# A packed square of attention probabilities for the second block of queries

## The reference

```python
nb = s // WINDOW                      # 2 blocks of 128 queries
kcat = concatenate([previous key block (zeros for the first), own key block])
scores = einsum('bnqkrd,bnjkd->bkrnqj', qb, kcat) * HEAD_DIM ** -0.5
dist = qi - kj + WINDOW
valid = (dist >= 0) & (dist < WINDOW) & (key_pos >= 0)
logits = where(valid, scores - slope * dist, -inf)
m = maximum(max(logits), sink)
pexp = exp(logits - m)
probs = pexp / (sum(pexp) + exp(sink - m))
out = einsum('bkrnqj,bnjkd->bnqkrd', probs, vcat)
```

## Time and profile before

| | us |
|---|---|
| median of 3 runs | 1937.97 (1937.92 to 1938.11) |
| the profiled execution | 1938.91 |
| its span | 1937.2 |
| TensorE busy | 1922.5 (99%) |
| VectorE busy | 1264.7 (65%) |
| ScalarE busy | 1084.3 (56%) |
| mean granted TensorE clock | 0.999 |

### The profile page before, as it was taken

How to read it: one execution, slowest core, us unless ns; L and a number is a source line. 1 busy time by engine, 2 the same in 40 slices (tenths; PEclk the granted TensorE clock), 3 DMA queues, 4 the chain that set the end, 5 groups by cost and what they waited for, 6 DMA issues and landing times.

```text
span 1937.2 us, 28994 instructions
## 1 busy us (share of the span) xinstructions
PE 1922.5 (99%) x10281; PEld 1634.9 (84%) x10281; DVE 1264.7 (65%) x1534; ACT 1084.3 (56%) x1474; POOL 33.5 (2%) x79
## 2 busy tenths in 40 slices
PE   9999999999999999999999999999999999999998
PEld 7888888888887878888888888888888888888886
DVE  6777788777868975545444555776776666744454
ACT  6566765777557764444344445666666666534443
POOL 1000000000000100000000000000000000000000
PEclk9999999999999999999999999999999999999999
DMA  7765666666654437666666565666666666666564
GB/s 225 211 191 166 197 205 183 186 174 204 195 163 131 131 123 215 194 190 197 194 191 194 178 228 192 200 188 186 191 189 193 186 184 189 190 200 194 193 195 142
DMA packets 294855, 362.05 MB, mean 187 GB/s; under 512 B 11073, under 2 KB 217985, under 8 KB 293377
## 3 DMA queue, kind: packets, MB, share of 16 engines
q1 hardware_dynamic: 294784, 361.12, 61.0%
HBM read 358.91 MB, written 2.16 MB: 186 GB/s over the span
## 4 chain that ended last, share of the span: by engine, by line
PE 98%; DVE 1%; ACT 1%; issue 0%; DMA 0%; DVEq 0%; SPq 0%; POOLq 0%; POOL 0%; ACTq 0%
PE ps L1381 35%; PE ps L1383 18%; PE ps L1366 14%; PE ps L1368 13%; PE ps L1367 13%; PE ps L1568 1%; PE ps L1496 1%; PE ps L1509 1%; PE ps L1520 0%; PE ps L1569 0%; PE ps L1557 0%; PE ps L1414 0%; DVE lo L851 0%; ACT hi L438 0%; PE ps L1436 0%
## 5 line engine op out<-in xcount | busy, mean ns | idle before, releaser
L851 DVE TENSOR_TENSOR lo<-raw,hi 128x1024 fp32r<-128x1024 f32 x658 | 801.5, 1224 | 520.3 <-ACT hi L438 514.2
L1381 PE MATMUL ps<-uHL,hi 128*128 128x512 f32 x2960 | 1041.9, 396 | 1.3 <-DVE uHL L863 1.0
L438 ACT ACTIVATE hi<-raw 128x1024 fp32r<-128x1024 f32 x658 | 688.7, 1055 | 519.6 <-PE ps L1368 386.5
L1383 PE MATMUL ps<-uHL,lo 128*128 128x256 f32 x2960 | 828.2, 280 | 0.0
L1381 PEld LDWEIGHTS ps<-uHL,hi 128*128 128x128 f32 x2960 | 554.7, 187 | 132.3 <-issue 5.0
L1383 PEld LDWEIGHTS ps<-uHL,lo 128*128 128x128 f32 x2960 | 558.9, 189 | 0.1
L1368 PE MATMUL ps<-hi,aL 128*128 128x512 f32 x384 | 149.5, 389 | 0.0
L1368 PE MATMUL ps<-hi,hL 128*128 128x512 f32 x352 | 136.9, 389 | 0.0
L1367 PE MATMUL ps<-lo,hH 128*128 128x512 f32 x352 | 136.9, 389 | 0.0
L1366 PE MATMUL ps<-hi,hH 128*128 128x512 f32 x352 | 136.9, 389 | 0.0
L443 ACT ACTIVATE hb<-ps 128x512 f32<-128x512 f32 x92 | 54.7, 595 | 124.1 <-PE ps L1383 124.1
(11 more groups left out here) (189 smaller groups left out, 1647.3 us busy)
## 6 DMA issues: line engine op xcount, KB each, us to landing
raw<-w_in SPq DMA_DIRECT2D x266, 512.0 KB, 4.3
raw<-w_ffn_in SPq DMA_DIRECT2D x176, 512.0 KB, 3.8
raw<-w_ffn_out SPq DMA_DIRECT2D x88, 512.0 KB, 4.3
raw<-w_ssm_out SPq DMA_DIRECT2D x64, 512.0 KB, 4.4
raw<-w_attn_out SPq DMA_DIRECT2D x32, 512.0 KB, 4.2
raw<-w_o SPq DMA_DIRECT2D x32, 512.0 KB, 4.4
rows_b<-cum_rows SPq DMA_DIRECT2D x8, 1024.0 KB, 6.5
x_tok<-x SPq DMA_DIRECT2D x8, 256.0 KB, 5.4
```

Source lines behind the costliest of these rows:

```text
L438: act.activation(hi[:, s % SLOTS, :], raw[:, s % SLOTS, :], ACT.Copy).then_inc(hi_ready, 1)
L851: ve.tensor_tensor(lo[:, s % SLOTS, :], raw[:, s % SLOTS, :], hi[:, s % SLOTS, :].bitcast(F32), ALU.subtract).then_inc(lo_ready, 1)
L1381: pe.matmul(ps[:, pair + c, :], w_hi, uHL[:, kk].rearrange("p a n -> p (a n)"), start=kk == 0, stop=False)
L1383: last = pe.matmul(ps[:, pair + c, 0:SEQ], w_lo, uHL[:, kk, 0, :], start=False, stop=kk == k - 1)
```

## The change

In the second block of queries the two triangles complement each other. After the logits, the element-wise maximum of the previous-key block and the own-key block is written over the previous-key block (masked places lie far below every logit), so one 128x128 square holds all the logits of a row. Maximum, exponential, sum and normalisation work on that square, and so do the transposes: four for six. ScalarE copies the transposed square to `pT`, and VectorE then makes both triangles of it with two multiplies by masks (`att_masks`), before `values`, whose code is unchanged. A new semaphore `pt_kept` leads from ScalarE's copy to VectorE; `pt_ready` now comes from VectorE. `att_masks` of an iteration stands behind `lo_of` of the odd unit: iterations 0, 1 behind units 5, 7, iterations 2, 3 behind units 1, 3 of the next group (9 and 11 at the end). The last `values` moves from before unit 11 to before unit 13, its keep and the last piece of `attn_hi` from units 11 and 13 to 16, and the last pieces of `branch_lo` from units 12 and 13 to 13 and 17.

```diff
@@ att_exps (ScalarE)
-                    act.activation(lg[:, i, j, 0:P], lg[:, i, j, 0:P], ACT.Exp, bias=S[:, 1, 2 * j:2 * j + 1],
-                                   accum_out=S[:, 3, 2 * j:2 * j + 1])
-                    act.activation(lg[:, i, j, P:3 * P], lg[:, i, j, P:3 * P], ACT.Exp, bias=S[:, 1, 2 * j + 1:2 * j + 2],
-                                   accum_out=S[:, 3, 2 * j + 1:2 * j + 2])
+                    for b in range(2):
+                        n = 2 * j + b
+                        act.activation(lg[:, i, j, b * P:(b + 1) * P], lg[:, i, j, b * P:(b + 1) * P], ACT.Exp,
+                                       bias=S[:, 1, n:n + 1], accum_out=S[:, 3, n:n + 1])
@@ att_turned (ScalarE)
-                act.activation(pT[:, i % 2], ps[:, M + 2:M + 4, :].rearrange("p b n -> p (b n)")[:, 0:6 * P],
-                               ACT.Copy).then_inc(pt_ready, 1)
+                act.activation(pT[:, i % 2].rearrange("p (j n) -> p j n", j=2)[:, :, 0:2 * P],
+                               ps[:, M + 2, :].rearrange("p (j n) -> p j n", j=2), ACT.Copy).then_inc(pt_kept, 1)
@@ merge units (ScalarE)
+                elif u == 12:
+                    attn_hi(2)
+                elif u == 16:
                     att_keep(KVH - 1, 3)
-                elif u < 14:
                     act.drain()
-                    attn_hi(u - 10)
+                    attn_hi(3)
@@ VectorE
+            def packed(i):
+                return lg[:, i, :, 0:2 * P].rearrange("p j (b n) -> p j b n", b=2)
+
+            def att_masks(h, i):
+                ve.wait_ge(pt_kept, h * 4 + (i + 1))
+                p = pT[:, i % 2].rearrange("p (j c n) -> p j c n", j=2, c=3)
+                ve.tensor_tensor(p[:, :, 2, :], p[:, :, 1, :], triu[:, None, :].to_broadcast([P, 2, P]), ALU.mult)
+                ve.tensor_tensor(p[:, :, 1, :], p[:, :, 1, :], strict[:, None, :].to_broadcast([P, 2, P]),
+                                 ALU.mult).then_inc(pt_ready, 1)
@@ att_logits (VectorE)
+                ve.tensor_tensor(lg[:, i, :, P:2 * P], lg[:, i, :, P:2 * P], lg[:, i, :, 2 * P:3 * P], ALU.max)
+                ve.drain()
                 mx = pairs(S[:, 0, :])
-                ve.tensor_reduce(mx[:, :, 0:1], lg[:, i, :, 0:P], op=ALU.max, axis=AX.X)
-                ve.tensor_reduce(mx[:, :, 1:2], lg[:, i, :, P:3 * P], op=ALU.max, axis=AX.X)
+                ve.tensor_reduce(mx[:, :, :, None], packed(i), op=ALU.max, axis=AX.X)
@@ att_probs (VectorE)
-                r = pairs(S[:, 5, :])
-                ve.tensor_tensor(lg[:, i, :, 0:P], lg[:, i, :, 0:P], r[:, :, 0:1].to_broadcast([P, 2, P]), ALU.mult)
-                ve.tensor_tensor(lg[:, i, :, P:3 * P], lg[:, i, :, P:3 * P], r[:, :, 1:2].to_broadcast([P, 2, 2 * P]),
+                ve.tensor_tensor(packed(i), packed(i), pairs(S[:, 5, :])[:, :, :, None].to_broadcast([P, 2, 2, P]),
                                  ALU.mult).then_inc(probs_ready, 1)
@@ VectorE's order
+            def att_mask_side(h, u, older=True):
+                if u in (1, 3) and older:
+                    att_masks(h - 1, u // 2 + 2)
+                if u in (5, 7):
+                    att_masks(h, u // 2 - 2)
...
                     att_first(h, u)
                     lo_of(U_Q + u, h * Q_UN)
+                    att_mask_side(h, u)
                     q_rest(h, u)
...
-                if 10 <= u < 14:
-                    i = u - 10
+                if u in (10, 11, 13, 17):
+                    i = (10, 11, 13, 17).index(u)
@@ turn_probs (TensorE)
-                    for c in range(3):
-                        o = (3 * j + c) * P
-                        last = pe.transpose(ps[:, M + 2 + o // 512, o % 512:o % 512 + P],
-                                            lg[:, i, j, c * P:(c + 1) * P], ident[:])
+                    for c in range(2):
+                        o = (2 * j + c) * P
+                        last = pe.transpose(ps[:, M + 2, o:o + P], lg[:, i, j, c * P:(c + 1) * P], ident[:])
@@ merge units (TensorE)
-                    elif u == 11:
+                    elif u == 13:
                         values(KVH - 1, 3)
```

More of the change, by code:

```diff
@@ L230, in build @@
                                                           sem("probs_turned"), sem("pt_ready"))
-        pv_done, attn_out = sem("pv_done"), sem("attn_out")
+        pt_kept, pv_done, attn_out = sem("pt_kept"), sem("pv_done"), sem("attn_out")
         sv_ready, z_scaled, rows_landed, rows_used = sem("sv_ready"), sem("z_scaled"), sem("rows_landed"), sem("rows_used")
@@ L1173, in _ @@
                 lo_of(U_Q + u, 0)
+                att_mask_side(0, u, older=False)
                 if u == 1:
@@ L1212, in _ @@
                 if u < 8:
+                    att_mask_side(KVH - 1, u)
+                elif u in (9, 11):
+                    att_masks(KVH - 1, u // 2 - 2)
+                if u < 8:
                     q_rest(KVH - 1, u)
```

## The result

| | before | after |
|---|---|---|
| median of 22 runs, us | 1938.3 (1937.79 to 1939.16) | 1941.67 (1940.02 to 1942.92) |
| the profiled execution, its span | 1938.91, 1937.2 | 1941.75, 1940.0 |
| granted clock, mean | 0.999 | 0.998 |

The ratio is 1.0016, interval 1.001 to 1.0021: 3.4 us slower. The interval lies clear of 1, but the difference is under the 0.2% (3.9 us) that the prediction names as what this measurement can tell, so it counts as no change. The 22 times of after lie in two groups with nothing between 1940.59 and 1941.10: seven from 1940.02 to 1940.59 and fifteen from 1941.10 to 1942.92. Before has no such gap. The profiled run belongs to the upper one. The mean granted clock of the whole run is 0.999 in all seven runs of the lower group and 0.998 or less in fourteen of the fifteen of the upper one, a value that only 9 of 87 later runs of before show.

The account below looks back on a forecast made before the run. TensorE was taken as the bound, with VectorE saturated. VectorE's 7 x 0.51 = 3.57 us, with -0.05 and -0.03, made +3.5; less 1.1 for transposes, +2.4: 1940.4 us, own range 1939.2 to 1942.2, whole range 1937.2 to 1943.1.

Parts of the forecast that it names:

- part 1: TensorE's transposes: two fewer in each of 16 iterations, 0.22 us each, remove 3.5 us, all on the path.
- the rival of hidden masks: Masks cause no TensorE stall and the transposes' gain arrives: -3.5 and -0.37 us, 1934.1 us; chance 0.10.
- no spare: VectorE in the attention stretch: iteration mean 7.93 us, about 8.1 with gaps, against TensorE's 8.11.
- parts 2 to 4: VectorE per iteration: normalisation -0.34, added maximum +0.17, two masks +0.68; sum +0.51 us, bounds 0.34 and 0.77.
- The rival of more such gaps: VectorE's issue: added waits, drains and masks bring two 0.17 us gaps per iteration; +4.8, 1942.8 us; chance 0.16.
- part 5: Masks behind VectorE's odd unit, before `values`: 0.76 us must fit into 0.13 us, so TensorE stalls.
- Shift at `values` (0,0) +2.1: First iteration of group 0: `values` starts 2.1 us later, behind a new stall of 2.7 us.
- VectorE's entry into group 1: At lo of the odd unit at 620.66, VectorE is shifted by only -0.05 us; the first stall is absorbed.
- `values` (2,2), +3.5: After seven VectorE iterations at 0.51 us (3.57), `values` in group 2 starts 3.5 us later.
- From there to the end, -1.1: Without aL subtractions masks come in time; five groups of transposes still give 5 x 0.22 = 1.1 us.
- by the row the sum stays +2.4: Behind the first stall: the clock stayed up at 1.30 us idle, so no clock cost is added to +2.4.
- The rival's mechanism: Clock falls to half behind the first stall, unit 4 takes 2.9 us more; +4.7, 1942.7 us; chance 0.04.

Follow-up runs that it names:

- e1: The changed kernel plus 22 transposes into a free PSUM bank ahead of the first `values`, in TensorE's stall; 1940.14 us, ratio 1.0011.
- e7: The kernel before with four of six transposes per iteration, the third of each head left out and nothing put in its place; 1935.88 us, ratio 0.9989.
- e2: The changed kernel plus 22 matmuls of 256 columns into a free PSUM bank ahead of the first `values`; 1940.23 us.
- e5: The changed kernel with both mask multiplies on GpSimd instead of VectorE; 1938.85 us, ratio 1.0004.
- e10: The changed kernel with the eight aL pieces of the state-space branch spread over three head groups instead of two; 1940.87 us, ratio 1.0015.
- e3: The changed kernel with VectorE's masks ahead of the odd unit's lo instead of behind it; 1939.76 us, ratio 1.001.
- e8: The changed kernel with one more VectorE multiply per iteration ahead of the masks, into a tile nothing reads; 1945.22 us, ratio 1.0036.

## Why the prediction was right, and with what

The median of 1941.67 lies 1.3 above the forecast, in its own range; the sign and the mechanism are those of the forecast. But the kernel in which its chain of steps can be read is e1, without the fall of the clock: forecast +2.4, stretch +2.20, 1940.14 us against 1940.4. That these two times lie so close is in part luck: e1 is 1.9 us above its own runs of before (1938.22), and the forecast stood on a median of three runs, 1937.97, 0.3 below that of the 22.

**Transposes (part 1).** 64 transposes, 604.15 to 604.51 = 0.36 us of queue per group, 0.21 less (predicted 0.22). That 16 x 0.22 = 3.5 are on the path was wrong: only about 2.0 to 2.2 arrive even with nothing added (e7). The sum used the 0.22 only five times at the end, where it holds, so that the error did not reach it. It made the rival of hidden masks, 1934.1, too good: e7, with no masks at all, came to 1935.88. The queue of the transposes is 0.21 shorter, but a whole iteration without a wait only 0.17 (7.94 us against the 7.89 of the sum). And "no spare" was a little too strong: VectorE's seven iterations before took 56.07 us, 8.01 each against TensorE's 8.11.

**VectorE's sum (parts 2 to 4).** One normalisation of 0.69 holds 625.29 - 624.68 = 0.61 where two held 0.95: -0.34, as predicted. The masks hold 0.34 and 0.33, start at lo + 1.14, and are predicted to the hundredth. The maximum costs 628.15 - 627.65 = 0.50 up to the reduction, less 0.34: +0.16 (0.17). So this iteration grew from 7.63 to 8.14 us, +0.51. Over the seven it is 680.59 - 621.25 = 59.34 for 56.07: +0.467 each, as in e1 (679.09 - 619.76 = 59.33). The term was 0.04 too large: before's seven iterations held 0.6 us of issue gaps on L991 (0.09 each) that the trace of after does not have in 614 to 680; against it the maximum takes 0.52 instead of 0.42 in the iterations with the query step (L997). The rival of more such gaps has the opposite sign here.

**The place (part 5).** First stall 2.7 us: 2.73. Shift at `values` (0,0) +2.1: +2.20. VectorE's entry into group 1, -0.05: in e1 619.76 - 579.94 = 39.82 against 620.66 - 580.90 = 39.76, +0.06, so the stall is absorbed there. In after it is 621.25 - 579.84 = 41.41, +1.65: with the lower clock it is not. `values` (2,2), +3.5: +3.26 in e1, +4.87 in after. From there to the end, -1.1: -1.06 in e1, -1.04 in after.

**The clock.** This is the step that failed: "by the row the sum stays +2.4", chance 0.04. At 1.30 us of idleness the clock had stayed; that said nothing of 2.73. It fell in the profiled run, and by the two groups of times and the runs' mean clocks in some 14 or 15 of 22. The rival's mechanism came on top of the forecast, and it cost 1.6 us rather than 2.3. The Trainium skill's rule (TensorE: Matmul & The Clock Gate, "What's actually happening"), that the clock halves after idleness, is borne out by the 0.51 behind the stall. The other half, in "Part 4: PE-mode transpose", that transposes don't count as work for the clock, is not borne out here: in the profile of e1 transposes alone fill the stall and it stays at 1.00, as with matmuls in e2. The chance of 0.04 had been worked out as if a row at half the idle time were evidence.

**What would show it.** Waits for masks 6 to 7 us in all, longest 2.7: 5.8 and 2.7. None behind 682: the last is 0.23 at 682.53. VectorE at 95% or more in 614 to 680: 94%. An iteration near 8.4: 59.34 / 7 = 8.48. `values` near 682.2: 682.53.

## What to carry to other kernels

Before taking work from the busiest engine, look in the order of time at the stretch where it happens: a second engine at 93% took back the gain and more, and half a us per iteration added there is paid once for each iteration in which it has no slack. The two need not meet directly: in e7 and e5 VectorE's pace reached TensorE through a third engine's step that stood behind a wait for VectorE. A new stall has a price beyond its length if the clock falls behind it, and a trace that shows shorter idleness with the clock up says nothing of that; independent work in the stall tells the two apart in one run. Of the versions tried, those with transposes left out aside, none is faster than the kernel before; the best, with `values` a unit later, is 0.02% slower by its median, at most 0.11% by its interval.

## What the runs showed of the hardware

- Idle 2.73 us, TensorE came back at a granted clock of 0.51 and 0.63 for some 4 us in the profiled run (after; 0.57 and 0.58 in e10), by the times in most runs but not in all. After 1.55 us (e3) and 1.30 us (before) the profiled runs show 1.00. After 3.06 us (e8) it came back at full pace and the clock fell only behind that: 0.98 in 598 to 600, 0.50 and 0.67 in the 4 us behind.
- 22 fp32 transposes of 128x128 take 2.56 us back to back, 0.11 each.
- A multiply of 128x256 fp32 takes 738 to 756 ns on GpSimd (means) and 420 on VectorE. In e5 a VectorE operation on 128x4 that began during one on GpSimd ended with it, within 0.03 us: 0.48 to 0.74 us where most of that was left, 0.17 where it was about to end, against 163 ns without.
- The same instructions ahead of the attention took 579.8 to 580.9 us from run to run. Two profiled runs can thus not be compared by their spans within 1 us; by stretches they can.
